# Four extra expert weight slots moved over buffers that die together, and taken in the order they come free

## The chip, the cores and the metric

One core of a Trainium2 chip runs one program. The metric is the device time of an execution in microseconds. TensorE (PE) multiplies, VectorE (DVE) and ScalarE (ACT) do the element work, and SyncE's queue (SP) issues nearly every transfer. GpSimd does nothing that matters here.

## What is computed

A decoder trunk of two layers on 256 tokens of width 1024, all in float32. Cut to what matters:

```python
for layer in range(2):
    h = rms_norm(x, attn_norm_g[layer])
    cols = h @ w_in[layer]                    # three token mixers share this projection
    mix = concat(norm(mla(cols)), norm(swa(cols)), norm(stick(cols)))
    x = x + mix @ w_out[layer]
    h = rms_norm(x, ffn_norm_g[layer])
    if layer == 0:
        x = x + swiglu(h, dense_gate, dense_up, dense_down)      # hidden width 2816
    else:
        x = x + moe_swiglu(h, router_w, moe_gate, moe_up, moe_down)  # 8 experts, top 2, hidden width 3584
```

The eight experts' weights are 8 x 3 x 1024 x 3584 x 4 bytes, 352 MB, of the 415 MB that the core reads in all. Each is read once.

## The kernel before

**Weights come in units.** A unit is a block of 128 partitions x 4096 floats, 2 MB. `ring` has 7 slots of one unit. The 30 units of the two mixers and the dense layer (`UNITS`) go through it in order, unit `no` in slot `no % 7`. An expert is 21 units (`MOE_UNITS`): for each chunk of 1024 hidden columns the gate's two, the up projection's two, then the down units of the chunk before. The last chunk is 512 wide. Eight experts make 168 units, numbered n = 0 to 167 here. A unit is loaded by one DMA that SP issues at L513. On the SBUF side it is written in runs of 8 KB (most of the down units), 4 KB (gate and up of 1024 columns) or 2 KB (gate and up of 512 columns) per partition.

**Eleven slots for the experts.** Beside `ring`, the experts use `more_ring`, four slots more (L316). `moe_slot_no` (L381) gives unit n the slot n % 11 of a list in which places 0 to 6 are `ring`'s and places 7 to 10 are `more_ring`'s. So in the stream of loads, seven go to `ring`, then four to `more_ring`, and so on round.

**What a load waits for.** SP works in order (L486 to L514). Loads n = 0 to 6 wait until DVE has split the last piece of the unit that was in that `ring` slot (L497): the last dense unit, the four `w_in` units of layer 1, and its two `w_out` units. Loads n = 7 to 10 wait for the last matmul of layer 1's output projection, `("piece", 1, N_OUT - 1)` (L495), since `more_ring` lies over memory that the mixers and this projection use. From n = 11 on a load waits for PE to be done with unit n - 11 (L491 to L493).

**The output projection** multiplies in eight pieces (`N_OUT`), q = 0 to 7. Each piece of weights is split into a high and a low part in one of four half slots: `d_hi_01`/`d_lo_01` serve pieces 0, 1, 4 and 5, `d_hi_23`/`d_lo_23` pieces 2, 3, 6 and 7. The activations are in `hid_hi` and `hid_lo`.

**The experts on PE.** For each expert PE gathers its tokens with a one-hot matrix `pick` (L862), multiplies the 21 units (L903 in halves of the array, L918 in strips), and scatters the result (L996, L1002) while the next expert runs. Four of the experts, 0, 3, 5 and 7, have room for fewer tokens and leave out L918. The next expert's gather stands before the last units of an expert. `pick` (L319) is written by DVE at L1811.

**Memory.** Tensors are laid one behind the other, each start rounded up to 32 bytes per partition. After the small tensors of the whole program come either `mixer_consts`, `uq`, `ukv` and the buffers of the mixers and the dense layer (L279 to L312), or, over the same bytes, `more_ring`, `xgT`, `hidT`, `pick`, `pick_g` and `y` (L313 to L321). `small` holds the small weights of both layers and the router's.

Of the kernel before, what the change touches and what calls it, by code (L numbers as in the profile page):

```python
# [30 lines left out]
P = 128  # L31
D = 1024
T = 256
TT = T // P
KD = D // P
DEPTH = 2
HD = 64
QR, KVR, NOPE, ROPE = 256, 128, 64, 32
HA, HB, HKV, HC = 4, 8, 2, 4
QK = NOPE + ROPE  # L40
# [18 lines left out]
GROUP = P  # L59
# [3 lines left out]
_at = 0  # L63
# [5 lines left out]
N_CONST = _at  # L69
N_KEPT = CONST["cos"][0]  # L70


SMALL = {}
_at = 0
for _l in range(DEPTH):
    for _name, _w in (("attn_g", KD), ("ffn_g", KD), ("out_g", KD), ("cq_g", 2), ("ckv_g", 1), ("swa_q_g", 1),
                      ("swa_k_g", 1), ("qn_g", QK), ("kn_g", QK), ("sinks", HB)):
        SMALL[_name, _l] = (_at, _w)
        _at += _w
SMALL["router"] = (_at, KD * NE)  # L80
N_SMALL = _at + KD * NE

RING = 7
UNIT = KD * CH
# [10 lines left out]
N_UNITS = len(UNITS)  # L95
# [7 lines left out]
MOE_UNITS.append(("d", NCH - 1, 0))  # L103
M_UNITS = len(MOE_UNITS)
MORE_SLOTS = 4
M_RING = RING + MORE_SLOTS
assert M_UNITS % RING == 0

# [3 lines left out]
PER_UNIT = UNIT // PIECE  # L112
# [63 lines left out]
BIG, LITTLE = 3, 2  # L176
# [38 lines left out]
class Counts:  # L215
# [6 lines left out]
    def at(self, key, it=None, back=0):  # L222
        if self.known is None:
            return 1 if it is None else it + 1
        name, loop, start, m = self.known[key]
        if loop is None:
            return m
        k = self.known["per", loop, name]
        if it is None:
            return start + (self.known["trips", loop, name] - 1) * k + m  # L230
        assert start + m - back * k > 0
        return it * k + (start + m - back * k)
# [10 lines left out]
def trunk_program(nc, known, x, cst, smalls, w_in, w_uq, w_ukv, w_out, dense_g, dense_u, dense_d, moe_g, moe_u,  # L243
# [3 lines left out]
    with ExitStack() as ctx:  # L247
        def sb(name, shape, dt=F32):
            return ctx.enter_context(nc.sbuf_tensor(name, shape, dt))

        def sem(name):
            return ctx.enter_context(nc.semaphore(name))
# [4 lines left out]
        small = sb("small", [P, N_SMALL])  # L257
# [24 lines left out]
        with ExitStack() as trunk:  # L282
# [3 lines left out]
            with ExitStack() as stage:  # L286
                def sb_stage(name, shape, dt=F32):
                    return stage.enter_context(nc.sbuf_tensor(name, shape, dt))
# [24 lines left out]
        with ExitStack() as stage:  # L313
            def sb_stage(name, shape, dt=F32):
                return stage.enter_context(nc.sbuf_tensor(name, shape, dt))
            more_ring = sb_stage("more_ring", [P, MORE_SLOTS, UNIT])  # L316
            xgT = sb_stage("xgT", [P, KD, GROUP])
            hidT = sb_stage("hidT", [P, 2, BIG * 2 * P])
            pick = sb_stage("pick", [P, TT, GROUP])  # L319
            pick_g = sb_stage("pick_g", [P, TT, 2 * P])  # L320
            y = sb_stage("y", [P, BIG * T])[:, :]  # L321


        probsT = hT[:, :, :].rearrange("p k t -> p (k t)")[:, 0:4 * SEG].rearrange("p (h s) -> p h s", h=4)
# [36 lines left out]
        pe_done, act_done, dve_done = sem("pe_done"), sem("act_done"), sem("dve_done")  # L361
        pe_p, act_p, dve_p = (Progress(n, marks) for n in ("pe", "act", "dve"))
        at = counts.at
# [3 lines left out]
        first_loaded = [sem(f"first_loaded{r}") for r in range(KD // 2 - 1)]  # L367
        slot_loaded = [sem(f"slot_loaded{n}") for n in range(M_RING)]
        last_y, last_scatter = sem("last_y"), sem("last_scatter")
# [10 lines left out]

        def moe_slot_no(g, s, n):  # L381

            l = (s * M_UNITS + n) % M_RING if g == 0 else n % RING
            return (N_UNITS + l) % RING if l < RING else l

        def moe_slot(g, s, n):
# [3 lines left out]
        def moe_loaded(g, s, n, it=None):  # L390
# [3 lines left out]
            if g == 0:  # L394
                return slot_loaded[l], 16 * (used + (s * M_UNITS + n) // M_RING + 1)
            used += sum(moe_slot_no(0, *divmod(m, M_UNITS)) == l for m in range(NE * M_UNITS))
# [48 lines left out]
        @block.sync  # L445
        def _(sp):
            for a in range(TT):
                sp.dma_start(xres[:, a, :], x[0, a * P:(a + 1) * P, :]).then_inc(x_loaded, 16)
            sp.dma_start(ident, cst[:, 0:P]).then_inc(ident_loaded, 16)
            sp.dma_start(small[:], smalls[:]).then_inc(small_loaded, 16)  # L450

            def load_up(l):
                sp.dma_start(uq[:], w_uq[l].rearrange("(k p) n -> p k n", p=P)).then_inc(up_loaded, 16)
                sp.dma_start(ukv[:], w_ukv[l]).then_inc(up_loaded, 16)

            def free(no):

                kind, l, n = UNITS[no - RING]
                if kind == "in":
                    return dve_done, at(("in_rest", l, IN_PIECES.index((n, KD // 2 - 1))))  # L460
                return dve_done, at(("rest", l, L_LAST[l][kind, n]))

            for no, (kind, l, n) in enumerate(UNITS):
                if no >= RING:
                    sp.wait_ge(*free(no))
                dst, src = unit_source(kind, l, n, slot_of(no))
                if no == 0:
                    for r in range(KD // 2 - 1):
                        sp.dma_start(dst[:, 2 * r:2 * r + 2, :], src[:, 2 * r:2 * r + 2, :]).then_inc(first_loaded[r], 16)
                    dst, src = dst[:, KD - 2:, :], src[:, KD - 2:, :]  # L470
                sp.dma_start(dst, src).then_inc(slot_loaded[no % RING], 16)
                if no == 1:
                    sp.dma_start(consts[:, P:], cst[:, P:N_KEPT]).then_inc(const_loaded, 16)
                    sp.dma_start(mixer_consts[:], cst[:, N_KEPT:]).then_inc(const_loaded, 16)
                    load_up(0)
                if no == UNIT_NO["down", 0, 0]:
                    sp.wait_ge(pe_done, at(("up_proj", 0)))
                    load_up(1)

            def expert_units(g):  # L480

                for n in range((ROUNDS if g else 1) * NE * M_UNITS):
                    s, m = divmod(n, M_UNITS)
                    kind, c, h = MOE_UNITS[m]
                    if g:
                        if n >= RING:  # L486
                            before_s, before_m = divmod(n - RING, M_UNITS)
                            sp.wait_ge(pe_done, at((g, None, "unit", before_m), before_s))
                        else:
                            sp.wait_ge(pe_done, at((0, NE - 1, "unit", M_UNITS - 1)))  # L490
                    elif n >= M_RING:  # L491
                        before_s, before_m = divmod(n - M_RING, M_UNITS)
                        sp.wait_ge(pe_done, at((g, before_s, "unit", before_m)))  # L493
                    elif n >= RING:
                        sp.wait_ge(pe_done, at(("piece", DEPTH - 1, N_OUT - 1)))  # L495
                    else:
                        sp.wait_ge(*free(N_UNITS + n))  # L497
                    rank = s % NE if g else RANK_AT[s]
                    if rank == 0:
                        e = slice(0, 1)  # L500
                    elif m == 0:
                        sp.wait_ge(dve_done, at("order"))
                        e = bass.ds(sp.value_load(order[0:1, rank:rank + 1], min_val=0, max_val=NE - 1), 1)
                    if kind == "d":
                        src = moe_d[0, e, c * CH:(c + 1) * CH, :]
                    else:
                        rows, cols = UNIT // GU_COLS[c] * P, slice(c * 2 * CH, c * 2 * CH + GU_COLS[c])
                        src = (moe_g if kind == "g" else moe_u)[0, e, h * rows:(h + 1) * rows, cols]
                    if kind == "d" and c < NCH - 1:
                        src = src.rearrange("o (v p e) n -> p (o v) (e n)", p=P, e=2)  # L510
                    else:
                        src = src.rearrange("o (k p) n -> p (o k) n", p=P)
                    sp.dma_start(moe_slot(g, s, m).rearrange("p (k n) -> p k n", n=src.shape[-1]), src).then_inc(  # L513
                        slot_loaded[moe_slot_no(g, s, m)], 16)  # L514

            expert_units(0)
            sp.wait_ge(dve_done, at("overflow"))
            more = sp.value_load(over_i[0:1, 0:1], min_val=0, max_val=1)
            with sp.If(more > 0):
                expert_units(1)  # L520
            for q in range(2 * TT):
                a, part = q // 2, slice(q % 2 * CH, (q % 2 + 1) * CH)
                sp.wait_ge(result_ready, q + 1)
                sp.dma_start(out[0, a * P:(a + 1) * P, part], xres[:, a, part]).then_inc(out_stored, 16)
            sp.wait_ge(out_stored, 16 * 2 * TT)
# [1436 lines left out]
```

## Time and profile before

| | us |
|---|---|
| median of 3 timed runs (lowest to highest) | 1276.07 (1273.01 to 1276.68) |
| the profiled execution's own time | 1271.22 |
| its span, first to last instruction | 1269.4 |
| PE busy in the span | 1242.1 (98%) |
| DVE busy, ACT busy | 344.2, 307.6 |
| mean share of time in which the 16 DMA engines worked on the main queue | 83.0% |

The page divides the span into 40 slices of 31.7 us. PE is busy in all of them. The DMA row is low in slices 3 to 13, where weights are few, and 9 in every slice from the 15th to the end, at about 410 GB/s. TensorE's granted clock over the span is 0.997 of full speed, so nearly the whole run is at the 2.4 GHz level. Times in the rows below are microseconds from the span's start.

### The profile page before, as it was taken

The page shows a single profiled execution, that of the slowest core. Times are in us where ns is not written, and L with a number is a line of the kernel's source. Part 1 is how long each engine was busy: PE and PEld are TensorE (multiplying, and loading weights), DVE is VectorE, ACT ScalarE, POOL GpSimd, SP SyncE. Part 2 cuts the span into 40 slices and gives each one's busy share as a digit, 9 for nine tenths or more (in the row PEclk, how much of TensorE's full clock was granted, in tenths as well). Part 3 has the DMA queues.
Part 4 walks back from the last instruction along what each step waited for, and adds up shares of the span by engine and source line. Part 5 has one row for each costly group of instructions (what it writes and reads, how often), then busy time and mean ns, then how long its engine had stood idle before and what let it go on. Part 6 is the DMA issues. An engine that isn't in the chain of part 4 may idle for free.

```text
span 1269.4 us, 20546 instructions
## 1 busy us (share of the span) xinstructions
PE 1242.1 (98%) x9126; PEld 729.3 (57%) x9126; DVE 344.2 (27%) x680; ACT 307.6 (24%) x687; POOL 0.2 (0%) x4
## 2 busy tenths in 40 slices
PE   7999999999999999999999999999999999999996
PEld 6778999998878734444544353353454343445333
DVE  5678654655677610100010001001001001000100
ACT  5676543444577400000100010000000000000000
POOL 0000000000000000000000000000000000000000
PEclk9999999999999999999999999999999999999999
DMA  9923543366510799999999999999999999999995
GB/s 354 386 100 133 198 172 128 133 207 245 199 68 30 297 409 412 410 420 410 416 416 412 418 389 374 409 418 415 413 415 417 418 408 419 415 416 413 418 416 214
DMA packets 114892, 417.65 MB, mean 329 GB/s; under 512 B 3440, under 2 KB 8176, under 8 KB 102512
## 3 DMA queue, kind: packets, MB, share of 16 engines
q1 hardware_dynamic: 114800, 416.29, 83.0%
q8 instruction: 74, 1.21, 0.4%
q14 instruction: 18, 0.15, 0.0%
HBM read 415.23 MB, written 1.05 MB: 328 GB/s over the span
## 4 chain that ended last, share of the span: by engine, by line
PE 89%; DVE 5%; DMA 2%; ACT 2%; SPq 1%; issue 1%; DVEq 0%; ACTq 0%
PE ps L903 44%; PE ps L918 12%; PE ps L573 7%; PE ps L575 7%; PE ps L574 7%; PE ps L862 2%; DMA ring<-moe_d 2%; PE ps L949 2%; PE ps L996 1%; DVE xres L1407 1%; DVE scratch L1525 1%; PE ps L701 1%; SPq L513 1%; DVE d_lo L1667 1%; PE ps L706 1%
## 5 line engine op out<-in xcount | busy, mean ns | idle before, releaser
L903 PE MATMUL ps<-ring,xgT 128*64 128x512 f32 (+1 forms) x1328 | 249.2, 527 | 1.3 <-issue 1.3
L903 PEld LDWEIGHTS ps<-ring,xgT 128*64 128x64 f32 x1328 | 94.3, 137 | 143.6 <-issue 129.7
L1845 DVE TENSOR_TENSOR hT<-ps,hT 128x512 f32<-128x512 f32 (+3 forms) x32 | 23.7, 742 | 545.4 <-PE ps L903 484.6
L903 PE MATMUL ps<-more_ring,xgT 128*64 128x512 f32 (+1 forms) x720 | 149.8, 566 | 1.3 <-DMA more_ring<-moe_u 1.3
L903 PE MATMUL ps<-ring,hidT 128*64 128x512 f32 x608 | 137.3, 596 | 3.5 <-DMA ring<-moe_d 3.5
L1667 DVE TENSOR_TENSOR d_lo<-ring,d_hi 128x1024 fp32r<-128x1024 f32 x82 | 99.7, 1223 | 77.3 <-ACT d_hi L1263 77.1
L1305 ACT ACTIVATE hidT<-ps 128x512 f32<-128x512 f32 (+3 forms) x32 | 20.4, 637 | 393.3 <-PE ps L949 210.7
L1263 ACT ACTIVATE d_hi<-ring 128x1024 fp32r<-128x1024 f32 x82 | 85.8, 1062 | 99.2 <-PE ps L575 99.2
L903 PEld LDWEIGHTS ps<-more_ring,xgT 128*64 128x64 f32 x720 | 50.7, 137 | 91.7 <-issue 88.9
L573 PE MATMUL ps<-hT_hi,d_hi 128*128 128x256 f32 x352 | 99.7, 283 | 0.0
L575 PE MATMUL ps<-hT_hi,d_lo 128*128 128x256 f32 x352 | 99.6, 283 | 0.0
L574 PE MATMUL ps<-hT_lo,d_hi 128*128 128x256 f32 x352 | 99.6, 283 | 0.0
L903 PEld LDWEIGHTS ps<-ring,hidT 128*64 128x64 f32 x608 | 42.3, 137 | 83.0 <-issue 81.1
L1302 ACT ACTIVATE hT<-ps 128x512 f32<-128x512 f32 (+3 forms) x32 | 20.4, 637 | 279.6 <-PE ps L903 240.7
L574 PEld LDWEIGHTS ps<-hT_lo,d_hi 128*128 128x128 f32 x352 | 67.6, 192 | 0.2
L573 PEld LDWEIGHTS ps<-hT_hi,d_hi 128*128 128x128 f32 x352 | 67.6, 192 | 0.2
L575 PEld LDWEIGHTS ps<-hT_hi,d_lo 128*128 128x128 f32 x352 | 67.5, 192 | 0.0
L918 PE MATMUL ps<-ring,xgT 128*32 128x256 f32 (+1 forms) x1344 | 66.1, 345 | 0.0
L903 PE MATMUL ps<-more_ring,hidT 128*64 128x512 f32 x288 | 64.9, 595 | 0.0
L573 PE MATMUL ps<-d_hi,hid_hi 128*128 128x512 f32 x152 | 59.8, 393 | 0.0
L574 PE MATMUL ps<-d_lo,hid_hi 128*128 128x512 f32 x152 | 59.2, 390 | 0.0
L575 PE MATMUL ps<-d_hi,hid_lo 128*128 128x512 f32 x152 | 59.2, 389 | 0.0
(249 smaller groups left out, 1347.1 us busy)
## 6 DMA issues: line engine op xcount, KB each, us to landing
ring<-moe_d SPq DMA_DIRECT2D x38, 2048.0 KB, 20.1
ring<-moe_u SPq DMA_DIRECT2D x37, 2048.0 KB, 23.6
ring<-moe_g SPq DMA_DIRECT2D x33, 2048.0 KB, 24.0
more_ring<-moe_g SPq DMA_DIRECT2D x23, 2048.0 KB, 23.2
more_ring<-moe_u SPq DMA_DIRECT2D x19, 2048.0 KB, 23.2
more_ring<-moe_d SPq DMA_DIRECT2D x18, 2048.0 KB, 22.7
ring<-w_in SPq DMA_DIRECT2D x6, 2048.0 KB, 10.5
ring<-dense_g SPq DMA_DIRECT2D x5, 2048.0 KB, 7.8
```

The source lines that it names most:

```text
L573: pe.matmul(out, hi_l, hi_r, start=start, stop=False, skip_group_check=True)
L574: pe.matmul(out, hi_l, lo_r, start=False, stop=False, skip_group_check=True)
L575: return pe.matmul(out, lo_l, hi_r, start=False, stop=stop, skip_group_check=True)
L862: ins = pe.matmul(ps[:, 6 + k // 4, k % 4 * P:(k % 4 + 1) * P], xn[:, a, k * P:(k + 1) * P], pick[:, a, :], start=a == 0, stop=a == TT - 1 ...
L903: ins = pe.matmul(ps[q * HALF:(q + 1) * HALF, b0, 0:wide], x, w[:, i * cols + q * wide:i * cols + (q + 1) * wide], start=first, stop=last, ...
L918: ins = pe.matmul(ps[q * STRIP:(q + 1) * STRIP, b0 + b, c0:c0 + wide // 2], x, w[:, i * cols + q * wide // 2:i * cols + (q + 1) * wide // ...
L949: ins = pe.transpose(ps[:, b, j % 4 * P:(j % 4 + 1) * P], part, ident)
L1263: nc.scalar.activation(hi_of(q), slot_of(no)[:, r * PIECE:(r + 1) * PIECE], ACT.Copy).then_inc(act_done, act_p.step(("lead", l, q)))
L1302: nc.scalar.activation(sig[:, 0:w], ps_flat[:, 0:w], ACT.Silu).then_inc(act_done, act_p.step((g, s, "silu", c)))
L1305: nc.scalar.activation(hidT[:, c % 2, 0:w], ps_flat[:, b0:b0 + w], ACT.Copy).then_inc(act_done, act_p.step((g, s, "hidT", c)))
L1667: nc.vector.tensor_tensor(lo_of(q), slot_of(UNIT_NO[kind, l, c])[:, r * PIECE:(r + 1) * PIECE], hi_of(q).bitcast(F32), ALU.subtract).then_ ...
L1845: nc.vector.tensor_tensor(hid[:, 0:w], ps_flat[:, 2 * CH:2 * CH + w], sig[:, 0:w], ALU.mult).then_inc(dve_done, dve_p.step((g, s, "hid", c)))
```

## The change

`more_ring` is moved behind `xgT`, `hidT` and `pick_g`, and behind a spacer, `beside_picks`, whose width makes it begin where `hid_hi` (and the mixers' `mla_T`) begins. Its first slot then lies over `hid_hi` and `hid_lo`, its second over `d_hi_01` and `d_lo_01`, its third over `hT_hi` and `hT_lo` (in the mixers: over `cols` and the start of `scratch`), its fourth over `d_hi_23` and `d_lo_23`. `xgT`, `hidT` and `pick_g` come to lie over the mixers' constants and `uq`, `ukv`. `pick` is no tensor of its own any more: it is laid over the first 256 columns of `small`, where the mixers' small weights were; the `ffn_g` weights are moved behind them so that they stay.

A new list, `SLOT_ORDER`, gives the order of slots: `ring` 0 to 4, then `more_ring`'s third, `ring` 5, `more_ring`'s second, `ring` 6, `more_ring`'s first, `more_ring`'s fourth. The four slots get three kinds of wait: the last value product of the sliding-window heads (`("oB", 1, 7)`) for the third, piece 5 (`PER_UNIT + 1`) for the second, the last piece as before for the other two.

```diff
-    for _name, _w in (("attn_g", KD), ("ffn_g", KD), ("out_g", KD), ("cq_g", 2), ...
+    for _name, _w in (("attn_g", KD), ("out_g", KD), ("cq_g", 2), ...
         SMALL[_name, _l] = (_at, _w)
         _at += _w
+N_MIXER_SMALL = _at
+for _l in range(DEPTH):
+    SMALL["ffn_g", _l] = (_at, KD)
+    _at += KD
...
 MORE_SLOTS = 4
+SLOT_ORDER = (0, 1, 2, 3, 4, RING + 2, 5, RING + 1, 6, RING, RING + 3)
+assert N_MIXER_SMALL >= TT * P
...
-            more_ring = sb_stage("more_ring", [P, MORE_SLOTS, UNIT])
             xgT = sb_stage("xgT", [P, KD, GROUP])
             hidT = sb_stage("hidT", [P, 2, BIG * 2 * P])
-            pick = sb_stage("pick", [P, TT, GROUP])
             pick_g = sb_stage("pick_g", [P, TT, 2 * P])
+            sb_stage("beside_picks", [P, N_CONST - N_KEPT + 2 * HA * QK + HA * (NOPE + HD) - KD * GROUP - 2 * BIG * 2 * P - TT * 2 * P])
+            more_ring = sb_stage("more_ring", [P, MORE_SLOTS, UNIT])
             y = sb_stage("y", [P, BIG * T])[:, :]
+        pick = small[:, 0:TT * P].rearrange("p (a n) -> p a n", a=TT)
...
-            l = (s * M_UNITS + n) % M_RING if g == 0 else n % RING
+            l = SLOT_ORDER[(s * M_UNITS + n) % M_RING] if g == 0 else n % RING
...
-                    elif n >= RING:
+                    elif SLOT_ORDER[n] == RING + 2:
+                        sp.wait_ge(pe_done, at(("oB", DEPTH - 1, HB - 1)))
+                    elif SLOT_ORDER[n] == RING + 1:
+                        sp.wait_ge(pe_done, at(("piece", DEPTH - 1, PER_UNIT + 1)))
+                    elif SLOT_ORDER[n] >= RING:
                         sp.wait_ge(pe_done, at(("piece", DEPTH - 1, N_OUT - 1)))
                     else:
-                        sp.wait_ge(*free(N_UNITS + n))
+                        sp.wait_ge(*free(N_UNITS + SLOT_ORDER[n]))
```

## Rows read from the trace of the kernel before

**Rows 1.** The page: the span, and the chain that ended last.

```profile
span 1269.4 us, 20546 instructions
PE 89%; DVE 5%; DMA 2%; ACT 2%; SPq 1%; issue 1%; DVEq 0%; ACTq 0%
```

**Rows 2.** PE's timeline at the end: start, duration, line, [idle before, its releaser].

```profile
1241.42 3.67 PE L903 MATMUL ps<-more_ring,xgT 128*64 128x256 f32 x32 [1.30 <-DMA more_ring<-moe_u]
1246.41 3.65 PE L903 MATMUL ps<-ring,hidT 128*64 128x512 f32 x16 [1.32 <-DMA ring<-moe_d]
...
1251.33 3.65 PE L903 MATMUL ps<-ring,hidT 128*64 128x512 f32 x16 [0.90 <-DMA ring<-moe_d]
1256.31 3.65 PE L903 MATMUL ps<-ring,hidT 128*64 128x512 f32 x16 [1.33 <-DMA ring<-moe_d]
1260.87 2.00 PE L996 MATMUL ps<-y,hT 64*128 64x256 f32 x16 [0.90 <-ACT y L1332]
```

**Rows 3.** SP's timeline: the issues of loads n = 5 to 11, by start.

```profile
408.47 0.37 SPq L513 DMA_DIRECT2D ring<-moe_g  x1
...
422.52 0.37 SPq L513 DMA_DIRECT2D ring<-moe_u  x1
428.01 0.37 SPq L513 DMA_DIRECT2D more_ring<-moe_u  x1
...
429.49 0.64 SPq L513 DMA_DIRECT2D more_ring<-moe_g  x1
447.98 0.37 SPq L513 DMA_DIRECT2D ring<-moe_g  x1
```

**Rows 4.** DMA issues at 428.01, 429.49 and 447.98: KB each, us from issue to landing.

```profile
more_ring<-moe_u SPq DMA_DIRECT2D x1, 2048.0 KB, 7.5
...
more_ring<-moe_g SPq DMA_DIRECT2D x1, 2048.0 KB, 22.0
ring<-moe_g SPq DMA_DIRECT2D x1, 2048.0 KB, 8.6
```

**Rows 5.** PE's timeline: last value product, last matmul of piece 5, expert 0's first.

```profile
404.07 0.39 PE L709 MATMUL ps<-cols,hT 128*128 128x64 f32 x2
...
420.95 0.39 PE L575 MATMUL ps<-d_hi,hid_lo 128*128 128x512 f32 x1
...
444.30 0.65 PE L903 MATMUL ps<-ring,xgT 128*64 128x512 f32 x2 [1.27 <-issue]
```

**Rows 6.** Engines' busy time by stretch; last three columns: PE's clock, DMA share, GB/s.

```profile
750.00:760.00 10.00, 10.00 (x111) 6.43 (x109) 1.13 (x4) 1.63 (x5) 0.00 (x0) 1.00 1.01 396
760.00:770.00 10.00, 10.00 (x72) 3.45 (x70) 0.00 (x0) 0.81 (x1) 0.00 (x0) 1.00 0.78 285
```

**Rows 7.** SP's timeline: the issues that close two more_ring runs and two ring runs.

```profile
1079.26 10.24 SPq L513 DMA_DIRECT2D ring<-moe_u  x1
...
1100.53 5.76 SPq L513 DMA_DIRECT2D more_ring<-moe_g  x1
...
1139.78 0.45 SPq L513 DMA_DIRECT2D ring<-moe_u  x1
...
1161.46 4.76 SPq L513 DMA_DIRECT2D more_ring<-moe_u  x1
```

**Rows 8.** DMA issues: the four of Rows 7 in the same order, us to landing last.

```profile
ring<-moe_u SPq DMA_DIRECT2D x1, 2048.0 KB, 30.0
...
more_ring<-moe_g SPq DMA_DIRECT2D x1, 2048.0 KB, 28.5
...
ring<-moe_u SPq DMA_DIRECT2D x1, 2048.0 KB, 24.9
...
more_ring<-moe_u SPq DMA_DIRECT2D x1, 2048.0 KB, 23.0
```

**Rows 9.** Main queue: packets, MB, share; 4 KB runs: 1163.2-1181.6 (more_ring), 1142.9-1161.8 (ring).

```profile
q1 hardware_dynamic: 1932, 7.68, 101.8%
...
q1 hardware_dynamic: 1936, 7.71, 101.7%
```

**Rows 10.** The same, 8 KB runs: 542.7-551.0 (more_ring), 572.5-581.0 (ring).

```profile
q1 hardware_dynamic: 458, 3.53, 101.0%
...
q1 hardware_dynamic: 471, 3.59, 101.6%
```

More of the change, by code:

```diff
@@ L75 @@
 for _l in range(DEPTH):
-    for _name, _w in (("attn_g", KD), ("ffn_g", KD), ("out_g", KD), ("cq_g", 2), ("ckv_g", 1), ("swa_q_g", 1),
+    for _name, _w in (("attn_g", KD), ("out_g", KD), ("cq_g", 2), ("ckv_g", 1), ("swa_q_g", 1),
                       ("swa_k_g", 1), ("qn_g", QK), ("kn_g", QK), ("sinks", HB)):
```

## The prediction

> **What bounds the kernel now.** I read the page first. PE carries 89% of the chain that ended last and transfers carry 2% [rows 1], and PE is busy nearly everywhere, so this looks like a kernel bound by PE. The second view corrects that: PE's timeline at the end. From 1241 us on PE stops ahead of each of the last units until that unit's transfer lands, four times, 1.30 + 1.32 + 0.90 + 1.33 = 4.85 us, and the last unit's matmuls begin at 1256.31, just behind the last landing [rows 2]. What follows (the last products, the last y, scatter, adds, output) is a fixed tail of some 13 us to 1269.4. So the end of the run is the landing of load n = 167 plus that tail. PE is close behind: had every unit been there in time, only 4.85 us would go.
>
> The third view is the queue itself. Is it working all the time before that last landing? By stretches, its share is about 1.0 from 428 us on with one hole, between 760 and 770, where it is 0.78 against 1.01 before it, some 2.3 us idle [rows 6]. There the eleven slots were full and SP waited for PE. So the experts have two stretches: one up to 768, in which the queue works off its backlog and then waits for PE, and one from 768 to the last landing at 1256, 488 us without a gap. In the second the time is the number of loads times the time of one. Nothing won before 768 crosses it; everything that a load costs more behind it arrives at the end in full.
>
> **Part 1: the early loads.** SP now issues n = 5 at 408.47, n = 6 at 422.52, n = 7 to 10 from 428.01 on, and n = 11 at 447.98 [rows 3]. The new conditions: the last value product begins at 404.07, so n = 5 goes at about 404.5; n = 6 takes the `ring` slot that n = 5 had, 408.5; piece 5 has its last matmul at 420.95, so n = 7 goes at 421.3; n = 8 at 422.5; n = 9 and 10 at 428.0 [rows 3, 5]. Two loads of six are 10 us earlier. But n = 11 waits for PE to be done with unit 0, which begins at 444.30 [rows 5] for reasons that no load enters (router, sorting, gather). Now n = 10 lands at 429.49 + 22.0 = 451.5 and n = 11 at 447.98 + 8.6 = 456.6, right behind it [rows 3, 4]. After the change n = 10 lands at about 444, the queue runs dry, and n = 11 is still issued at 447.98 and travels through an empty queue. That takes 7.5 (n = 7 met a nearly empty one) to 8.6 us [rows 4], so it lands at 455.5 to 456.6: 0 to 1.1 us earlier. The eleven slots eat the rest. PE does not start the experts earlier, and no load was late for it there. At most 1.1 us, and the hole at 768 takes it.
>
> The waits added on SP queue nothing of value behind them: what stands behind n = 5's is n = 6, which waits longer anyway. The four early loads run beside the output projection, whose splits on DVE and ACT already had loads n = 5 and 6 beside them. I take 0 for it (bounds 0 and +1 us); a delay of PE there would go through to the end, since the hole at 768 follows PE.
>
> **Part 2: `pick` over `small`, xgT, hidT and pick_g moved.** The same instructions in the same number. The columns under `pick` belong to the mixers, which are over by the time of the first `pick`. 0, bounds -0.3 and +0.3 us.
>
> **Part 3: where more_ring begins.** This is where the change costs. Adding up the tensors with each start rounded up to 32 bytes, `ring` begins 128 bytes past a multiple of 256 and `more_ring` begins exactly on one (145,792 bytes behind `ring`). Each slot is 16,384 bytes, so every slot of a ring has the offset of its ring. After the change `more_ring` begins 12,704 bytes further on, which is 160 bytes past a multiple of 256 and no longer a multiple of 64.
>
> Does that matter? The trace before holds both cases side by side in a saturated queue. A run of four loads into `more_ring` is enclosed by landings at 1079.26 + 30.0 = 1109.26 and 1100.53 + 28.5 = 1129.03: 4.94 us each. The seven `ring` loads behind it end at 1139.78 + 24.9 = 1164.68: 5.09 us each. The next four into `more_ring` end at 1161.46 + 23.0 = 1184.46: 4.95 us each [rows 7, 8]. The difference is 0.15 us a load. To take out the mixture of shapes I compare windows of one shape by queue time (window x share / MB x 2.097 MB). In 4 KB runs, `more_ring`: 18.4 x 1.018 / 7.68 gives 5.115 us a load; `ring`: 18.9 x 1.017 / 7.71 gives 5.228; difference 0.113 [rows 9]. In 8 KB runs: 8.3 x 1.010 / 3.53 gives 4.980 and 8.5 x 1.016 / 3.59 gives 5.045; difference 0.065 [rows 10]. Halving the number of runs roughly halves the difference, as a fixed cost for each run would; so 2 KB runs get twice the 4 KB value, 0.226. Over an expert's 13 loads of 4 KB, 6 of 8 KB and 2 of 2 KB the mean is (13 x 0.113 + 6 x 0.065 + 2 x 0.226) / 21 = 0.110 us.
>
> From 768 on nine of the fifteen `more_ring` rounds are left (n = 73 to 164), 36 loads. If the new place costs what `ring`'s place costs, the second stretch grows by 36 x 0.110 = 4.0 us (by shapes) to 36 x 0.15 = 5.4 us (by landings). The first stretch grows by 24 x 0.110 to 24 x 0.15 = 2.6 to 3.6 us; off it go the 2.3 us of the hole and up to 1.1 us of part 1, which leaves 0 to 1.3. The sum is 4.0 to 6.7 us. I take 5.0, the middle of the second stretch and a little of the first. Bounds: 0 if the difference between the rings has another cause, such as their place in memory; no row shows an offset that is an odd multiple of 32, so I let it cost up to twice `ring`'s, +11 us.
>
> The Trainium skill has a rule that speaks against this change. In "DMA: Bandwidth & Descriptors", section "How a descriptor splits into AXI transactions", it says by the vendor's account that a run which does not start on a multiple of 256 bytes has its first transaction start at the boundary below, and the bytes before the start still cost beats of 32 bytes. By that, 4 KB at offset 128 cost 132 beats for 128, and at offset 160 they cost 133. An estimate by that page for offset 160 is 5 beats more on 128 (3.9%), on 256 (2.0%) and on 64 (7.8%), of 4.94 us each: 0.19, 0.10 and 0.38 us, 0.18 on the mean, and 6.5 us on the 36 loads. The trace agrees in direction and in how it goes with the run's length [rows 8 to 10].
>
> **The sum.** Profiled execution: 1271.22 + 5.0 = 1276.2. The median of the timed runs is 4.85 above the profiled time, so I add the 5.0 to the median: 1281.0. If the timed runs have slower transfers than the profiled one, the hole is smaller there and more of the first stretch's growth comes through, which only adds.
>
> **Rivals.**
> - *Slower through the place of `more_ring`*, as above: +4 to +7, time 1280 to 1283. For: two kinds of measurement in the same queue. Against: it rests on one offset standing for another. Its worse form (the offset of 32 costs twice): +8 to +11, 1284 to 1287.
> - *The place costs nothing*, since the difference between the rings is due to something else, or is lost among the 16 engines. Then part 1 is left, -1.1 to 0: 1275.0 to 1276.1. For: the ring's seven loads and the four differ in more than an offset. Against: the scaling with the length of the runs.
> - *Faster: the lead survives* (the other side of no change). Two loads land 10 us earlier, and if the queue kept that lead up to n = 167, PE's waits at the end would go: 1276.07 - 4.85 = 1271.2. It decides at n = 11, which would have to be issued before 447.98, and at 768, where the queue must not be idle. For: the four waits of rows 2 are a real price. Against: n = 11 waits for PE [rows 3, 5], and the hole [rows 6].
>
> **How the numbers follow.** Changes under 0.3%, 3.8 us, can hardly be told from none. Place costs as computed: 0.50, of which a fifth comes out under 3.8 us; its worse form: 0.12. Costs nothing, or up to 3 us: 0.30. Faster through the lead: 0.08. Slower by over 0.3%: 0.40 + 0.12 and some of the scatter of the timed runs (1273.0 to 1276.7), 0.54; within 0.3%: 0.38; faster: 0.08. The range is 1274 to 1287: from no cost with a low draw to the worse form. The likeliest case's own range is 1279 to 1284.
>
> **What would show it.** Right: issues near 404.5, 408.5, 421.3, 422.5, 428 and again 447.98; a hole in the queue before 448; loads into `more_ring` no longer faster than those into `ring`; the hole at 760 to 770 smaller or gone; PE's idle time at the end grown from 4.85 to about 10 us, with the same tail. Wrong: `more_ring` loads still at 4.94 us; or n = 11 issued earlier; or PE's idle time at the end gone.

## The result and the profile after

| | before | after |
|---|---|---|
| median of the timed runs, us (19 each) | 1273.61 | 1279.47 |
| lowest to highest | 1270.12 to 1276.68 | 1276.10 to 1282.74 |
| profiled execution's span | 1269.4 | 1274.9 |

The ratio is 1.005 with a 95% interval of 1.0041 to 1.0060: slower by 6.4 us of 1273.6, between 5.2 and 7.6. The two medians lie 5.9 us apart. (The baseline here is the median of the nineteen runs taken beside the changed kernel; the 1276.07 of the first table was the median of three.)

PE's timeline at the end of the changed kernel, with the columns of [rows 2]; L914 is the old L903 and L1007 the old L996:

```profile
1226.08 3.65 PE L914 MATMUL ps<-ring,xgT 128*64 128x512 f32 x16 [0.63 <-DMA ring<-moe_u]
1231.14 3.65 PE L914 MATMUL ps<-more_ring,hidT 128*64 128x512 f32 x16 [1.41 <-DMA more_ring<-moe_d]
...
1236.15 3.65 PE L914 MATMUL ps<-ring,hidT 128*64 128x512 f32 x16 [0.46 <-DMA ring<-moe_d]
1241.54 3.67 PE L914 MATMUL ps<-more_ring,xgT 128*64 128x256 f32 x32 [1.74 <-DMA more_ring<-moe_g]
1246.92 3.67 PE L914 MATMUL ps<-more_ring,xgT 128*64 128x256 f32 x32 [1.71 <-DMA more_ring<-moe_u]
1251.90 3.65 PE L914 MATMUL ps<-ring,hidT 128*64 128x512 f32 x16 [1.31 <-DMA ring<-moe_d]
...
1256.87 3.65 PE L914 MATMUL ps<-ring,hidT 128*64 128x512 f32 x16 [0.95 <-DMA ring<-moe_d]
1261.83 3.65 PE L914 MATMUL ps<-ring,hidT 128*64 128x512 f32 x16 [1.31 <-DMA ring<-moe_d]
1266.39 2.00 PE L1007 MATMUL ps<-y,hT 64*128 64x256 f32 x16 [0.90 <-ACT y L1343]
```

Eight waits for a transfer stand where four stood in [rows 2], and they add up to 9.52 us against 4.85. The last unit begins at 1261.83, against 1256.31, and the tail behind it is the same 13.1 us.

SP's timeline around the early loads (columns of [rows 3]), and then the delay from issue to landing of the two issued at 428.55 and 448.11:

```profile
404.61 0.37 SPq L524 DMA_DIRECT2D more_ring<-moe_g  x1
408.59 0.37 SPq L524 DMA_DIRECT2D ring<-moe_u  x1
421.50 0.37 SPq L524 DMA_DIRECT2D more_ring<-moe_u  x1
422.66 0.37 SPq L524 DMA_DIRECT2D ring<-moe_d  x1
428.14 0.37 SPq L524 DMA_DIRECT2D more_ring<-moe_d  x1
428.55 0.47 SPq L524 DMA_DIRECT2D more_ring<-moe_g  x1
448.11 0.37 SPq L524 DMA_DIRECT2D ring<-moe_g  x1
```

```profile
more_ring<-moe_g SPq DMA_DIRECT2D x1, 2048.0 KB, 17.0
ring<-moe_g SPq DMA_DIRECT2D x1, 2048.0 KB, 7.5
```

The four early loads go out as the new conditions allow, and n = 11 still goes at 448.11 (before: 447.98), since PE starts the experts no sooner. It lands 7.5 us later, at 455.6 against 456.6; the load ahead of it, n = 10, had landed at 445.5, against 451.5 before.

Busy time by stretch in the changed kernel, the columns of [rows 6]; the last three are PE's clock, the DMA share and GB/s:

```profile
440.00:450.00 10.00, 8.73 (x55) 5.28 (x55) 4.63 (x34) 1.14 (x4) 0.00 (x0) 1.00 0.44 153
750.00:760.00 10.00, 10.00 (x113) 6.36 (x111) 1.13 (x4) 1.64 (x5) 0.00 (x0) 1.00 1.03 412
760.00:770.00 10.00, 10.00 (x72) 3.52 (x70) 0.00 (x0) 0.81 (x1) 0.00 (x0) 1.00 0.86 329
```

The share of 0.44 from 440 to 450 is the new hole: all eleven slots were full. The hole between 760 and 770 is still there, 0.86 in place of 0.78, so the lead of the start ends there, and so does most of what the first stretch lost: n = 70 lands 3.0 us later than before, n = 72 0.8 and n = 73 1.5 us later.

The queue in the second stretch, 150 us of it in each kernel, same columns. The kernel before:

```profile
1050.00:1200.00 150.00, 150.00 (x1329) 65.69 (x1327) 11.37 (x23) 10.13 (x18) 0.00 (x0) 1.00 1.02 417
```

After:

```profile
1050.00:1200.00 150.00, 150.00 (x1329) 65.82 (x1327) 11.36 (x23) 10.14 (x18) 0.00 (x0) 1.00 1.02 410
```

PE does the same work in it (1329 matmuls, 150 us busy), the queue is as busy as before (1.02), and it moves 410 GB/s in place of 417. That is the loss.

### The profile page after: what moved, and what is told of

Its sections match the earlier page's. It is cut to its first block, busy times and chain, and to the rows that moved or that the text cites. A ratio compares the mean times of both kernels' runs of the same rounds, so it can differ in the third digit from the quotient of the medians.

```text
span 1274.9 us, 20546 instructions
## 1 busy us (share of the span) xinstructions
PE 1243.1 (98%) x9126; PEld 729.9 (57%) x9126; DVE 344.2 (27%) x680; ACT 307.8 (24%) x687; POOL 0.2 (0%) x4
## 4 chain that ended last, share of the span: by engine, by line
PE 88%; DVE 5%; DMA 4%; ACT 2%; SPq 1%; issue 1%; DVEq 0%; ACTq 0%
PE ps L914 43%; PE ps L929 12%; PE ps L584 7%; PE ps L586 7%; PE ps L585 7%; PE ps L873 2%; DMA ring<-moe_u 2%; DMA ring<-moe_d 2%; PE ps L960 2%; PE ps L1007 1%; DVE xres L1418 1%; SPq L524 1%; DVE scratch L1536 1%; PE ps L712 1%; DVE d_lo L1678 1%
## 5 line engine op out<-in xcount | busy, mean ns | idle before, releaser
L914 PE MATMUL ps<-ring,xgT 128*64 128x512 f32 (+1 forms) x1280 | 246.8, 535 | 1.9 <-issue 1.3
L914 PEld LDWEIGHTS ps<-ring,xgT 128*64 128x64 f32 x1280 | 91.0, 137 | 144.5 <-issue 131.2
L914 PE MATMUL ps<-more_ring,xgT 128*64 128x512 f32 (+1 forms) x768 | 155.1, 550 | 3.4 <-DMA more_ring<-moe_g 1.7
L914 PE MATMUL ps<-ring,hidT 128*64 128x512 f32 x624 | 141.3, 595 | 4.0 <-DMA ring<-moe_d 4.0
L914 PEld LDWEIGHTS ps<-more_ring,xgT 128*64 128x64 f32 x768 | 54.3, 137 | 93.7 <-issue 89.2
L914 PEld LDWEIGHTS ps<-ring,hidT 128*64 128x64 f32 x624 | 43.7, 137 | 85.6 <-issue 83.6
L914 PE MATMUL ps<-more_ring,hidT 128*64 128x512 f32 x272 | 61.7, 595 | 1.4 <-DMA more_ring<-moe_d 1.4
## 6 DMA issues: line engine op xcount, KB each, us to landing
ring<-w_in SPq DMA_DIRECT2D x6, 2048.0 KB, 10.4
```

What stands on the lines that cost most here:

```text
L914: ins = pe.matmul(ps[q * HALF:(q + 1) * HALF, b0, 0:wide], x, w[:, i * cols + q * wide:i * cols + (q + 1) * wide], start=first, stop=last, ...
```

## The experiments

All shift tensors by padding and change nothing that is computed. They are compared with 1271.85, the median of the kernel before in the executions taken beside them. In each, "offset" means the bytes by which a ring's start lies past a multiple of 256.

**1. The changed kernel, with the place of `more_ring` put back on a multiple of 256.**

```diff
             ukv = trunk.enter_context(nc.sbuf_tensor("ukv", [P, HA * (NOPE + HD)], F32))
+            trunk.enter_context(nc.sbuf_tensor("pad_t", [P, 24], F32))
...
-            sb_stage("beside_picks", [P, ... - TT * 2 * P])
+            sb_stage("beside_picks", [P, ... - TT * 2 * P + 24])
```

> The changed kernel with 96 bytes of padding ahead of the output projection's buffers and of more_ring, so that more_ring begins on a multiple of 256 bytes again; order of slots, waits and pick over small stay. If the place of more_ring is the whole cost: loads into it take 4.94 us again instead of 5.09, and the time falls by about 6 us, to a ratio of 0.999 to 1.000 against the kernel before. If the early loads or pick over small cost anything, the ratio stays above: 1.005 if they are all of it.

The first padding moves the output projection's buffers along, so that the slots still lie over them.

Measured: 1272.03 against 1271.85, ratio 0.9998 (0.9986 to 1.0010). The queue in the same stretch:

```profile
1050.00:1200.00 150.00, 150.00 (x1329) 65.67 (x1327) 11.99 (x26) 10.13 (x18) 0.00 (x0) 1.00 1.02 418
```

96 bytes of padding take back the whole loss. New order, new waits and `pick` over `small` are all still there, so together they cost nothing and bring nothing that can be measured (the interval is 0.12% wide on either side).

**2. The kernel before, with only the place of `more_ring` moved to offset 160.**

```diff
+            sb_stage("pad_m", [P, 40])
             more_ring = sb_stage("more_ring", [P, MORE_SLOTS, UNIT])
```

> The kernel before with 160 bytes of padding ahead of more_ring and nothing else changed. If the place is the whole cost, this alone gives the changed kernel's time: ratio 1.004 to 1.006, PE's idle time at the end about 10 us in place of 4.85. If the cost is in the order, the waits or pick, the ratio is 1.000.

What lies behind `more_ring` (`xgT`, `hidT`, `pick`, `pick_g`, `y`) moves by the same 160 bytes.

Measured: 1278.45 against 1271.85, ratio 1.0047 (1.0032 to 1.0062).

```profile
1050.00:1200.00 150.00, 150.00 (x1328) 65.86 (x1329) 12.49 (x27) 9.69 (x18) 0.00 (x0) 1.00 1.03 410
```

The 160 bytes alone, without any other part of the change, give the changed kernel's time and its 410 GB/s. PE's eight waits for transfers at the end add up to 10.05 us in its trace. Experiments 1 and 2 are the two halves of one proof: removing the offset removes the loss, and adding it makes it.

**3. The kernel before, with both rings on a multiple of 256.**

```diff
+        sb("pad_f", [P, 32])
         ring = sb("ring", [P, RING, UNIT])
...
+            sb_stage("pad_m", [P, 32])
             more_ring = sb_stage("more_ring", [P, MORE_SLOTS, UNIT])
```

> The kernel before with ring moved by 128 bytes as well, so that both rings begin on a multiple of 256 bytes. If the place decides, ring's loads fall from 5.09 to 4.94 us too, 59 of them after 768 us, some 9 us of queue time; PE's idle time at the end was 4.85 us, so the time falls by 4 to 5 us, ratio about 0.9965, and then PE is the bound. If the difference between the rings was a matter of ring against more_ring, the ratio is 1.000.

Measured: 1267.47 against 1271.85, ratio 0.9959 (0.9946 to 0.9972), 5.2 us faster than the kernel before. The same stretch of the queue, then the end of its chain (start, duration, what was on it):

```profile
1050.00:1200.00 150.00, 150.00 (x1329) 65.78 (x1327) 11.37 (x23) 10.14 (x18) 0.00 (x0) 1.00 1.02 421
```

```profile
1213.22 20.75 PE ps L905 x96
1234.87 13.92 PE ps L905 x96
1249.16 7.04 PE ps L905 x32
1257.09 2.00 PE ps L998 x16
```

At 421 GB/s no transfer is left on the chain's end: PE works through to 1256 without one wait for a load. PE's 4.85 us of waits were all that could be gained, and the gain of 5.2 (3.6 to 6.9) is that. `ring`'s loads in 4 KB runs are now spaced by 4.97 us (median) in place of 5.11. So it was the offset, and not which of the two rings a load goes to.

**4. The changed kernel, with both rings on a multiple of 256.** The padding is 32 floats ahead of `ring` and 56 in place of experiment 1's 24.

> The changed kernel with both rings on a multiple of 256 bytes: the early loads with the cost of the place taken away. If the eleven slots eat the lead, as the prediction has it, this equals the kernel before with both rings aligned, ratio about 0.9965. If the early loads bring anything of their own, it is below that one by up to 1 us.

Measured: 1267.44, ratio 0.9964 (0.9950 to 0.9978).

```profile
1050.00:1200.00 150.00, 150.00 (x1329) 65.72 (x1327) 11.37 (x23) 10.39 (x19) 0.00 (x0) 1.00 1.02 421
```

The same as experiment 3. Where PE is the bound the early loads have nothing to give, and experiment 1 shows nothing of them where the queue is. Experiments 3 and 4 are the fastest versions of this case, ahead of both the kernel before and the changed one.

**5 to 8. Other offsets of `more_ring` in the kernel before**, one execution each, the padding of experiment 2 with 32, 8, 16 and 56 floats: offsets 128, 32, 64 and 224.

> The kernel before with more_ring 128 bytes past a multiple of 256, the offset that ring has. Loads into more_ring should then space exactly as ring's do: 5.12 us for 4 KB runs, 4.98 for 8 KB, 5.4 for 2 KB. One time only, near 1278 us.

> more_ring 32 bytes past a multiple of 256. If the cost grows with the bytes between the boundary below and the start (the page's beats: 1 more on 128), 4 KB loads take about 4.94 to 4.98 us. If any start off the boundary costs one fixed piece for each run, they take 5.12 us as at 128 and 160.

> more_ring 64 bytes past a multiple of 256. By growing cost, about 4.98 us for 4 KB loads; by a fixed cost, 5.12 us; if what counts is a multiple of 64, 4.9 to 4.95 us as on the boundary.

> more_ring 224 bytes past a multiple of 256. By growing cost (7 beats more on 128), 5.18 to 5.22 us for 4 KB loads, above ring's 5.12; by a fixed cost, 5.12 us.

The same stretch. Offset 32:

```profile
1050.00:1200.00 150.00, 150.00 (x1329) 65.81 (x1327) 11.37 (x23) 10.14 (x18) 0.00 (x0) 1.00 1.02 410
```

Offset 224:

```profile
1050.00:1200.00 150.00, 150.00 (x1333) 66.16 (x1331) 12.49 (x27) 10.17 (x20) 0.00 (x0) 1.00 1.02 410
```

All four give 410 GB/s (64 and 128 too), as 160 did. The median spacing of two landings in their traces, for loads written in 4 KB runs into `more_ring`, is 5.12 us at each of the offsets 32, 64, 128, 160 and 224, and 4.95 in the kernel before. The cost is the same at each of the five offsets, 32 bytes past as well as 224. The theory in which it grows with the bytes between the boundary and the start has fallen: it wanted 4.94 to 4.98 at 32, and over 5.18 at 224. That was the estimate from the Trainium skill's "DMA: Bandwidth & Descriptors", section "How a descriptor splits into AXI transactions", in which the beats grow with the offset; the measurement, on the side that is written, does not show that growth. What the landings support is one fixed piece more for each run. Between experiment 3 (both rings on the boundary) and experiment 2 (neither), the median spacing of all loads goes from 5.14 to 5.40 us in 2 KB runs, from 4.97 to 5.12 in 4 KB runs and from 4.90 to 4.98 in 8 KB runs: 0.26, 0.15 and 0.08, about half as much each time the number of runs halves. Why a run off the boundary takes longer is not shown by any of them.

Their times, 1281.24, 1277.26, 1281.96 and 1281.88 in that order, are single executions and are not ordered by the offset; the last section says what sets them apart.

## Why the prediction was right, step by step

**The time.** The forecast was 1276.07 + 5.0 = 1281.0, and 1279.47 was measured. The cost was 5.9 us by the medians and 6.4 by the ratio, so the 5.0 was too small, and the median that I started from, of three executions, lay 2.5 us above that of nineteen. The two errors partly cancel, and that part of the closeness is luck.

**What bounds the end.** Right: the last landing and a fixed tail. Four waits became eight, and the tail stayed at 13.1 us. PE is only 5 us behind as the next bound, which experiment 3 shows by running into it.

**The early loads: at most 1.1 us, taken by the hole at 768.** Right in every part that the sum uses: the issue times (404.6, 408.6, 421.5, 422.7, 428.1), n = 11 held by PE at 448.1, its landing 1.0 us earlier, and the hole at 760 to 770 still open. One sentence misread its own figures: not two of six loads were 10 us earlier, but one by 14 us and five by 1 to 7. Nothing was worked out from it, though the rival of the surviving lead repeats it. Experiment 1 puts the value of this part at nothing to within 0.12%, some 1.5 us, so the 1.1 us that it could have been at most is not excluded by it; the trace of the hole is what speaks against it.

**`pick` over `small` and the other moves.** Right, 0, by experiment 1.

**The place of `more_ring`.** Right in mechanism, by experiments 1 and 2. Its size in the profiled execution can be read behind the hole. SP issues n = 73 at 768.05 before; after the change the line is this one:

```profile
768.18 0.37 SPq L524 DMA_DIRECT2D more_ring<-moe_g  x1
```

Its delay from issue to landing, before and after:

```profile
more_ring<-moe_g SPq DMA_DIRECT2D x1, 2048.0 KB, 7.9
more_ring<-moe_g SPq DMA_DIRECT2D x1, 2048.0 KB, 9.3
```

PE's last unit begins 5.52 us later than before, and this splits up. n = 73 is issued 0.13 us later, and it takes 1.4 us longer to land. Half of that is the queue in front of it: n = 72 lands 3.0 us after n = 73's issue, against 2.3 before. From n = 72's landing to that of the last load, n = 167, it is 485.8 us before (770.4 to 1256.2) and 490.5 after (771.2 to 1261.7), 4.7 us more for 36 loads, 0.130 each. From n = 73's landing on it is 480.3 and 484.2, 4.0 us more for 35 loads, 0.114 each. So the value lies between the one by shapes (0.110) and the one by two short runs of landings (0.15).

One pair of traces does not settle it. The stretch from n = 73's landing takes 484.2 to 485.5 us in all six traces with `more_ring` off the boundary. But it takes 477.1 in experiment 1's trace, where `more_ring` is on it as in the kernel before, and no trace shows what sets these two 3 us apart. Experiments 3 and 4, with all slots on the boundary, have 472.7 and 473.5, and against the six that is 0.11 to 0.14 us for each of the 94 loads.

**The first stretch.** I allowed it 0 to 1.3 us and took about 0.3. It gave PE nothing: the changed kernel's PE is 0.13 us behind the old one at n = 11's issue and at n = 73's, and it is so already at n = 4's, which the change does not touch (361.74 against 361.61). What it gave is the queue in front of n = 73, 0.7 us, and up to all of the 1.4 us by which that load lands later. So the 5.0, made of 4.7 for the second stretch and 0.3 for the first, met 4.0 to 4.7 and 0.7 to 1.4. It was 0.4 low, and what it lacked is the first stretch's term, not the cost of a load. The timed runs lost 6.4 us (5.2 to 7.6), and that interval does not tell whether there is more of it in them.

**The worse form** (an offset of 32 past a multiple of 64 costs twice) did not happen: 128, a multiple of 64, and 160 cost the same.

**The rivals.** "The place costs nothing" fell with experiment 2. "The lead survives" fell twice: by the ratio of experiment 1, and by the changed kernel's own trace.

## What to carry to other kernels

When a change moves a buffer that a saturated queue writes, work out where the buffer starts. Here a multiple of 256 bytes was worth 0.08 to 0.26 us on a load of 5 us, by the length of its runs, and a re-layout lost it without a word about it in the code. Starting loads earlier brings nothing if a later point in the stream is set by the engine that frees the slots; look for the first load that waits for that engine, and for holes in the queue behind it. And where two buffers in one trace are served at two speeds, ask why before changing either: it told the loss in advance, and it pointed to the 5 us that the kernel before could still gain.

## What the runs showed of the hardware that was not expected

**The cost of an offset is flat.** 32, 64, 128, 160 and 224 bytes past a multiple of 256 all give 410 GB/s where four of eleven loads had been on the boundary at 417, and 421 with all of them on it.

**PE's stretches at half the clock set much of the difference between two executions.** Experiments 5 and 6 differ in an offset that the queue does not feel, and yet by 3.98 us. Their stretches around the router, the third column from the right being PE's granted clock. Experiment 6 (1277.26 us):

```profile
430.00:440.00 10.00, 8.76 (x45) 5.38 (x44) 5.99 (x30) 5.96 (x10) 0.00 (x0) 0.83 1.02 420
440.00:450.00 10.00, 8.74 (x54) 5.07 (x54) 4.64 (x34) 1.14 (x4) 0.00 (x0) 1.00 1.01 405
```

Experiment 5 (1281.24 us):

```profile
430.00:440.00 10.00, 8.29 (x46) 5.88 (x45) 5.66 (x26) 7.11 (x12) 0.00 (x0) 0.76 1.02 401
440.00:450.00 10.00, 8.73 (x45) 7.03 (x47) 3.37 (x17) 1.14 (x4) 0.00 (x0) 0.72 1.01 412
```

A mean of 0.83 over 10 us, made of the two levels 1 and one half, means 2 x 0.17 x 10 = 3.4 us at 1.2 GHz in experiment 6; in experiment 5 it is 2 x (0.24 + 0.28) x 10 = 10.4 us. Seven microseconds more at half speed are 3.5 us of PE's work at most. Ahead of the fall PE goes from the back-to-back matmuls of the output projection to the router's products of 8 columns, with gaps for ACT and DVE.

There is a second such stretch, at the start. A row of the same group of matmuls in experiment 6 and in experiment 5:

```profile
12.10 0.35 PE L575 MATMUL ps<-in_lo,in_hT_hi 128*128 128x416 f32 x1
12.03 0.55 PE L575 MATMUL ps<-in_lo,in_hT_hi 128*128 128x416 f32 x1
```

Experiment 5 keeps to the longer kind, one every 0.35 us in place of 0.19, until 15.4 us, and so it is 1.8 us behind when SP issues n = 4 (363.14 against 361.38). The router's stretch makes it 5.0 us at n = 11 (452.71 against 447.74), and n = 73 is still 5.0 us later. Of these 3.9 arrive at the last unit. How much arrives is not fixed: in experiment 1's trace PE was 2.56 us behind the kernel before at n = 73, and its last unit began only 0.14 us later. Experiments 7 and 8, both near 1282, show 0.74 and 0.75 in the two stretches.

The timed executions, each with its mean granted clock, show the same. Of the changed kernel's nineteen, the seven at 0.998 took 1276.10 to 1277.91 us, and the eleven at 0.994 to 0.996 took 1278.60 to 1282.74. Of the 29 of the kernel before taken beside the experiments, the eleven at 0.998 took 1269.36 to 1271.84 and the twelve at 0.995 or 0.996 took 1271.86 to 1276.28. So most of the scatter goes with the clock. At 0.998 alone the two kernels' medians are 1276.54 and 1270.59, 5.9 us apart, much as in the profiled pair. Whether padding has any part in which of the two an execution gets was not tried.
